# A split adaLN product: eight chunks ahead of the first norm, the others between the chunks of other matrices, in four strips of 32 columns

## What is computed

```python
c_act = jax.nn.silu(c)
for i in range(DEPTH):
    mod = (c_act @ ada_w[i] + ada_b[i])[:, None, :]          # (1024) @ (1024, 6144)
    sh1, sc1, g1, sh2, sc2, g2 = jnp.split(mod, ADA_CHUNKS, axis=-1)
    h = _rmsnorm(x, norm_mix_g[i]) * (1.0 + sc1) + sh1
    m = _conformer_conv(h, ...) if i == 0 else _stick_breaking_attention(h, ...)
    x = x + g1 * m
    h = _rmsnorm(x, norm_ffn_g[i]) * (1.0 + sc2) + sh2
    x = x + g2 * _peer(h, pk_w_q[i], pk_keys[i], pk_u[i], pk_v[i])
return _rmsnorm(x, final_g)
```

## Time and profile before

| | us |
|---|---|
| median of 3 runs | 3544.87 (3542.72 to 3547.4) |
| the profiled execution | 3545.07 |
| its span in the trace | 3543.3 |
| busy in the span: PE, DVE, POOL, ACT | 3179.2, 2502.8, 1254.0, 479.0 |
| mean granted TensorE clock | 0.921 |

### The profile page before, as it was taken

How to read it: one execution, slowest core, us unless ns; L and a number is a source line. 1 busy time by engine, 2 the same in 40 slices (tenths; PEclk the granted TensorE clock), 3 DMA queues, 4 the chain that set the end, 5 groups by cost and what they waited for, 6 DMA issues and landing times.

```text
span 3543.3 us, 44528 instructions
## 1 busy us (share of the span) xinstructions
PE 3179.2 (90%) x12852; PEld 2291.5 (65%) x12852; DVE 2502.8 (71%) x5303; ACT 479.0 (14%) x1062; POOL 1254.0 (35%) x1168
## 2 busy tenths in 40 slices
PE   7899869699999999999979897838999999999996
PEld 3685746596776766555568784737877676655554
DVE  0397899778888886666623586397788888766665
ACT  0211211010000000000043215201100000000001
POOL 0000000105555557777500000002255555677773
PEclk9899979659999999999979999975699999999998
DMA  8234315319999999999922340213399999999996
GB/s 313 87 133 170 114 64 180 131 32 388 410 403 409 406 406 410 410 410 410 372 84 97 118 143 12 85 59 100 114 410 407 406 401 409 405 410 410 410 410 262
DMA packets 242900, 957.18 MB, mean 270 GB/s; under 512 B 26953, under 2 KB 27129, under 8 KB 225146
## 3 DMA queue, kind: packets, MB, share of 16 engines
q0 software_dynamic: 147456, 536.94, 38.5%
q1 hardware_dynamic: 95354, 419.17, 31.2%
HBM read 953.90 MB, written 2.10 MB: 270 GB/s over the span
## 4 chain that ended last, share of the span: by engine, by line
PE 53%; DMA 16%; issue 12%; DVE 11%; ACT 4%; POOL 3%; DVEq 0%; POOLq 0%; ACTq 0%; SPq 0%
DMA v_rows<-in_pk_v,idx_now 14%; PE out_e L727 13%; PE acc L718 13%; PE acc L488 11%; PE mid L708 6%; PE acc L480 4%; DVE mod_rows L1290 2%; POOL v_rows L426 1%; DVE scratch L1309 1%; POOL u_rows L420 1%; DMA u_rows<-in_pk_u,idx_now 1%; PE mid L679 1%; PE out_e L510 1%; DMA weights<-in_ada 1%; DVE scratch L1306 1%
## 5 line engine op out<-in xcount | busy, mean ns | idle before, releaser
L727 PE MATMUL out_e<-weights,mod_rows 128*128 128x512 f32 x2048 | 932.4, 598 | 61.6 <-DVE mod_rows L1335 59.7
L718 PE MATMUL acc<-h_t,weights 128*128 128x256 f32 x4096 | 933.8, 381 | 0.0
L718 PEld LDWEIGHTS acc<-h_t,weights 128*128 128x128 f32 x4096 | 784.0, 192 | 217.8 <-issue 123.5
L426 POOL DMA_INDIRECT v_rows<-in_pk_v,idx_now x512 | 630.5, 1231 | 606.0 <-DVE mod_rows L1290 484.9
L1290 DVE SCALAR_TENSOR_TENSOR mod_rows<-v_rows,acts,mod_rows 128x1024 f32<-128x1024 f32 x512 | 657.9, 1285 | 199.0 <-DMA v_rows<-in_pk_v,idx_now 195.5
L1273 DVE SCALAR_TENSOR_TENSOR u_rows<-u_rows,h_rows 128x1024 f32<-128x1024 f32 x512 | 625.8, 1222 | 82.5 <-DMA u_rows<-in_pk_u,idx_now 81.7
L727 PEld LDWEIGHTS out_e<-weights,mod_rows 128*128 128x128 f32 x2048 | 377.2, 190 | 468.1 <-issue 368.0
L420 POOL DMA_INDIRECT u_rows<-in_pk_u,idx_now x512 | 564.6, 1103 | 292.4 <-issue 142.3
L415 POOL COPY idx_now<-pick_idx 128x8 int32 (+1 forms) x128 | 56.2, 439 | 1348.2 <-DVE pick_gate L1268 1300.5
L708 PEld LDWEIGHTS mid<-scratch 128*128 128x128 f32 x2048 | 338.6, 257 | 20.2 <-DVE scratch L1309 16.9
L708 PE MATMUL mid<-scratch 128*128 128x64 f32 x2048 | 341.4, 343 | 10.6 <-DVE scratch L1309 10.6
(11 more groups left out here) (184 smaller groups left out, 2072.0 us busy)
## 6 DMA issues: line engine op xcount, KB each, us to landing
weights<-in_u_t SPq DMA_DIRECT2D x256, 512.0 KB, 6.7
weights<-in_pk_v SPq DMA_DIRECT2D x256, 512.0 KB, 6.7
weights<-in_ada SPq DMA_DIRECT2D x42, 1024.0 KB, 4.9
weights<-in_pk SPq DMA_DIRECT2D x32, 1024.0 KB, 4.8
weights<-in_w_qkv SPq DMA_DIRECT2D x24, 1024.0 KB, 4.8
weights<-in_w_in SPq DMA_DIRECT2D x16, 1024.0 KB, 4.8
weights<-in_w_out SPq DMA_DIRECT2D x8, 1024.0 KB, 4.9
u_rows<-in_pk_u,idx_now POOLq DMA_INDIRECT x512, 10.9
```

The costliest lines, as they stand in the source:

```text
L426: nc.gpsimd.indirect_dma_start(v_rows[:, r % VR, :], None, a["pk_v"], bass.IndirectOffsetOnAxis(ap=idx_now[:, 1, par, r:r + 1], axis=0)).t ...
L718: last = nc.tensor.matmul(acc[s][:, 0:HALF], weights[:, s, k * P:(k + 1) * P], h_t[:, k, :], start=k == 0, stop=k == KB - 1)
L727: last = nc.tensor.matmul(out_e[2 * tt + c][:, :], e_act[:, s, tt * P:(tt + 1) * P], weights[:, s, D + c * 512:D + (c + 1) * 512], start=F ...
```

## The change

**The product in four strips.** `c_pad` is widened to windows of 32 columns, and `ada_rows` to all 128 partitions. The eight matmuls of a chunk no longer go to the same 24 rows: number `k` goes to the strip of 32 rows that begins at `k % 4 * 32`, by `tile_position`, so that row `n` of each of four strips gets a quarter of the sum of chunk `n`. The four are added where they are used: `strips`, a 128x32 tile that DVE makes once out of `ident`, takes the place of `ident` in `spread_columns` and in the picks of `spread_rows`, whose matmuls then run over 128 rows and not 24. The bias comes in by one matmul ahead of ACT's copy (`ada_bias_in`), and DVE's addition is gone.

**Layer 0 in two parts.** The first eight chunks (shift and scale of the first norm) stand ahead of everything: two through `weights`, six through `u_rows` and `v_rows`, whose DMAs SP now issues all at once, around the load of `x`. The other 16 stand two by two behind each `glu` chunk of half 0, in another PSUM tile (`out_e[1]`); their columns and rows are spread behind the second `glu` chunk of half 1.

**Layer 1 one by one.** Its 24 chunks stand each behind one chunk of `out` half 0 (4), `pk` half 0 (8), `out` half 1 (4) and `pk` half 1 (8), and none are left behind the last `pk`. DVE makes `mod_cols` of layer 1 behind the seventh `rank` of half 1, with the first softmax.

```diff
-ASIDE = 6
-ADA_PIECES = ((0, 4), (4, 4), (8, 2), (10, 2), (12, 12))
+STRIP = 32
+STRIPS = P // STRIP
+NOW = 8
+ASIDE = NOW - 2
-CHAIN = ([("ada", 0, 0, range(ADA_CHUNKS - ASIDE)),
-          ("glu", 0, 0, range(8)), ("glu", 0, 1, range(8)), ("ada", 1, 0, range(0, 4)), ("ada", 1, 1, range(4, 8)),
-          ("out", 0, 0, range(3)), ("ada", 1, 2, range(8, 10)), ("out", 0, 0, range(3, 4)), ("ada", 1, 3, range(10, 12)),
-          ("pk", 0, 0, range(8)), ("out", 0, 1, range(4)), ("pk", 0, 1, range(8)), ("ada", 1, 4, range(12, 24)),
+def beside(stage, half, count, first):
+    return [c for i in range(count) for c in ((stage, 0, half, i), ("ada", 1, 0, first + i))]
+CHAIN = ([("ada", 0, 0, 0), ("ada", 0, 0, 1)] +
+         [c for i in range(8) for c in (("glu", 0, 0, i), ("ada", 0, 0, NOW + 2 * i), ("ada", 0, 0, NOW + 2 * i + 1))] +
+         [("glu", 0, 1, i) for i in range(8)] +
+         beside("out", 0, 4, 0) + beside("pk", 0, 8, 4) + beside("out", 1, 4, 12) + beside("pk", 1, 8, 16) +
...
-            def ada_chunk(l, n, chunk):
-                window = ADA_CHUNKS - 1 - n
+            def ada_chunk(n, chunk, to, first):
+                window = STRIP - 1 - n
                 for k in range(KB):
-                    last = nc.tensor.matmul(out_e[0][0:ADA_CHUNKS, 0:NC], c_pad[:, k, window:window + ADA_CHUNKS],
-                                            chunk[:, k * NC:(k + 1) * NC], start=n + k == 0,
-                                            stop=n == ADA_CHUNKS - 1 and k == KB - 1)
+                    at = k % STRIPS * STRIP
+                    last = nc.tensor.matmul(to[at:at + STRIP, 0:NC], c_pad[:, k, window:window + STRIP],
+                                            chunk[:, k * NC:(k + 1) * NC], start=first and k < STRIPS, stop=False,
+                                            tile_position=(0, at))
...
             pe.wait_ge(c_pad_ready, 1)
-            ada(0, 0, ADA_CHUNKS - ASIDE)
+            for n in range(2):
+                ada(0, n, out_e[0], n == 0)
             for i in range(ASIDE):
                 pe.wait_ge(aside_in[i], 16)
-                last = ada_chunk(0, ADA_CHUNKS - ASIDE + i, aside[i])
+                last = ada_chunk(2 + i, aside[i], out_e[0], False)
             last.then_inc(aside_used, 1)
-            spread_columns(0)
+            ada_bias_in(0, out_e[0])
+            spread_columns(0, mid[0])
...
-            for i in range(4):
+            for i in range(8):
+                if i == 4:
+                    norm(0, 1, 0)
                 by_channel("glu", 0, 0, i)
-            norm(0, 1, 0)
-            spread_rows(0)
-            for i in range(4, 8):
-                by_channel("glu", 0, 0, i)
+                for n in range(NOW + 2 * i, NOW + 2 * i + 2):
+                    ada(0, n, out_e[1], n == NOW)
+            ada_bias_in(1, out_e[1])
             normed_columns(0, 1, 0)
             for i in range(8):
                 by_channel("glu", 0, 1, i)
+                if i == 1:
+                    spread_columns(1, mid[1])
+                    spread_rows(0)
             pe.wait_ge(rows_ready, 8)
             means(0, range(4))
-            ada(1, 0, 4)
             variance(0)
-            ada(1, 4, 4)
-            for i in range(3):
+            for i in range(4):
                 conv_out(0, i)
-            ada(1, 8, 2)
-            conv_out(0, 3)
-            ada(1, 10, 2)
+                ada(1, i, out_e[0], i == 0)
             norm(0, 0, 1)
             select(0, 0, {1: lambda: means(1, range(4)), 3: lambda: variance(1)})
             for i in range(4):
                 conv_out(1, i)
+                ada(1, 12 + i, out_e[0])
             norm(0, 1, 1)
             select(0, 1)
-            ada(1, 12, 12)
-            spread_columns(1)
+            ada_bias_in(2, out_e[0])
+            spread_columns(2, mid[0])
             peer(0)
```

More of the change, by code:

```diff
@@ L515, in ada @@
-            def ada(l, first, count):
-                if l and first == 0:
-                    pe.wait_ge(rows_ready, 8 * l)
-                for n in range(first, first + count):
-                    at = NUMBER["ada", l, 0, n]
-                    pe.wait_ge(weights_in[at % 2], 16 * (at // 2 + 1))
-                    ada_chunk(l, n, weights[:, at % 2, :]).then_inc(ada_used, 1)
-            def spread_columns(l):
-                pe.wait_ge(ada_ready, l + 1)
+                    at = k % STRIPS * STRIP
@@ L526, in spread_columns, with ada_bias_in @@
+            def ada_bias_in(part, to):
+                pe.wait_ge(bias_in, 32 if part == 2 else 16)
+                nc.tensor.matmul(to[:, 0:NC], ident[0:ADA_CHUNKS, :], ada_bias[:, :], start=False, stop=True
+                                 ).then_inc(ada_full, 1)
+            def spread_columns(part, to):
+                pe.wait_ge(ada_ready, part + 1)
+                pe.wait_ge(strips_ready, 1)
                 for c in range(2):
-                    last = nc.tensor.matmul(mid[0][:, c * ADA_CHUNKS:(c + 1) * ADA_CHUNKS], ada_rows[:, c * P:(c + 1) * P],
-                                            ident[0:ADA_CHUNKS, 0:ADA_CHUNKS], start=True, stop=True)
+                    last = nc.tensor.matmul(to[:, c * ADA_CHUNKS:(c + 1) * ADA_CHUNKS], ada_rows[:, c * P:(c + 1) * P],
+                                            strips[:, 0:ADA_CHUNKS], start=True, stop=True)
@@ L836, in norm @@
             def norm(l, h, which):
[L837 removed]
+                act.wait_ge(mod_ready, 3 if l else 1 + which)
                 act.wait_ge(rstd_ready, norm_no(l, h, which, 0) // 2 + 1)
```

107 lines of the change are left out of this document (55 added, 52 removed).

## The result

The changed kernel takes 3604.96 us (median of four executions, 3602.66 to 3606.15), against 3545.45 us for the kernel before in the same comparison (3542.72 to 3547.4): the ratio is 1.0168, 95% interval 1.0150 to 1.0185. It is 59.5 us slower. Direction and mechanism were forecast, the size (36 us) was not.

A forecast was written before the change was run, and what follows sets the result against it. Loads and adaLN products bound the start, then DVE's convolution and ranks; 83 us gained in front was to be lost in longer steps, `peer(0)` starting at 698.3 instead of 662.22: 3545 + 36 = 3581 us, range 3557 to 3605.

The forecast's parts named there:

- The front: Ahead of the first `glu` product: loads decide, and `glu` starts at 44.5 us instead of 127.76, 83 us ahead.
- a: PE's price of one adaLN chunk in four strips: taken as 1.8 us, between 0.9 side by side and 3.54 serial.
- A load whose place comes free late costs 5.0 us, the next one 2.6 more: Beside adaLN chunks: a load issued when its slot frees lands 5.0 us later; in `glu` the next load adds 2.6.
- The clock, 1.2 us a `glu` and `out` step and 1.5 in `pk`: PE returns slow after each load wait: 1.2 us added per `glu` and `out` step, 1.5 per `pk` step.
- the clock doesn't fall: Rival: no clock loss in the `glu`, `pk` and `out` steps and first scores, 25 us less, 3557 to 3562; chance 0.2.
- `out` of half 0 is covered by DVE, 2 us show: Layer 0, `out` of half 0: steps of 14.8 us, mostly hidden by DVE's half blocks between residuals; 2 us show.
- `pk` steps 13.4: `pk` of half 0: each step 6.91 + 5.0 + 1.5 = 13.4 us instead of 7.80; eight steps 109.6 instead of 71.8.
- First scores and ranks: `pk` of half 1: first scores after 25.9 us instead of 17.7; then DVE's ranks bind, 124.7 less 1.6 to `peer(0)`.
- Behind `peer(0)` nothing over 3 us: From 662 us on, after `peer(0)` starts: no term over 3 us, the rest follows as a block.
- The signs: Expected in the changed profile: `glu` steps 15 to 16 us, `centre` at 240 to 255, `peer`'s output at 680 to 720.
- hidden gaps (3517): Rival: exposed load gaps in `glu`, `pk` and `out` steps stay hidden, a chunk costing its 2.6 us transfer: 3517; chance 0.08.
- The fourth: Rival: strips run one after the other at 3.54 us a chunk and the clock falls in each gap: 3605 us; chance 0.17.

The follow-up runs named there:

- filled to the brim: Changed kernel with more matmuls of unread result added in the load gaps of layer 0's `glu`, `out` and `pk` steps: 3563.6 us.
- first experiment: Changed kernel with the eight products of an adaLN chunk put into one strip of 32 rows, one after the other: 3589.65 us.
- the kernel with the spare tiles: Changed kernel with adaLN chunks behind the second loaded through idle `u_rows`/`v_rows` tiles, layer 1's chunks distributed differently: 3477.15 us.
- one-strip version: The kernel with the spare tiles, but with the eight products of each adaLN chunk in one strip: 3577.04 us.
- the strips at their old places: Changed kernel with both layers' adaLN chunks back in the old order, keeping the four-strip product and what comes with it: 3501.97 us.

## Why the prediction came out as it did

**The front** (44.5 forecast, 45.99 measured): right. The eight chunks are bound by their loads; a = 1.07 instead of 1.8 changes nothing there.

**A load whose place comes free late costs 5.0 us, the next one 2.6 more**: right. The chain shows 4.6 to 5.0 us for `in_pk` and `in_w_out` (6.0 once), and in `glu` PE is back on a product 7.4 us after the last one ended (55.08 to 62.48; 7.3 to 8.4 in the others).

**The clock, 1.2 us a `glu` and `out` step and 1.5 in `pk`: this is the step that failed.** The mechanism was right, its price too low. I took it from one place, where 32 adaLN matmuls stood behind a wait of 2.96 us. In the changed kernel the eight `glu` products took 8.66 to 9.50 us, 9.17 in the mean, against 7.17 at full clock, so 2.0 (and the sum's base, 6.91, holds only for products in a row: 0.2 more a step); an `out` chunk took 11.85 us from its bias matmul at 295.82 to its adaLN chunk at 307.67, where it takes 8.55 with the gaps filled, so 3.3; a `pk` product 8.6 to 8.9 (and 10.08 once), mostly, so 1.7. Against the forecast that is 0.8 x 8 in `glu` and 0.4 to 2.1 in each `out` chunk, 12 to 13 in the seven on the path (three of half 0, four of half 1): about 19 of the 22.4 us; it is what grew in the table in the rows behind `glu` and behind the two `out`. The rival "the clock doesn't fall" put the sum's clock terms at 25 us (they make 27 on the path); taking the clock's fall away (filled to the brim) measured 39, and left 20 us over the kernel before, where that rival had 12 to 17.

The argument for the rival was wrong too: that adaLN products cut the gaps in two spoke, as I put it, for the full clock. At 1.07 us they are too short to do that. At 3.64 us they do (first experiment), which is why the one-strip kernel is faster: the tiling and the filling order work against each other. The Trainium skill, "TensorE: Matmul & The Clock Gate", section "HAM oscillation — how this bites in real kernels", describes the mechanism as throttling between bursts of matmuls separated by waits on DMA. The trace agrees: the granted clock is 0.81 in the `glu` steps, and 0.96 in the one-strip kernel and in the one filled to the brim (117 to 179 us). The bursts of that section are shorter than its waits; here they are longer, 8.7 to 9.5 us against some 4, and the clock fell all the same.

**`out` of half 0 is covered by DVE, 2 us show**: too little. With steps of 16.9 us DVE waited 22.6 us for four products (1.53, 3.28, 15.55 and 2.20) where it had waited 14.2, so 8.3 showed; 6.2 us of delay grew in that stage.

**`pk` steps 13.4**: right where a wait stood in them (13.7 to 13.9 in the last steps of half 0). Behind the means and the variance the load was hidden and the product ran at full clock, which the sum did not have, and the one at 406.71 ran at full clock too; so half 0 took 106.8 in all for 109.6. **First scores and ranks**: right; from `pk` of half 1 to the first `rank` 27.3 us for 25.9, and from there 122.8 for 123.1.

**Behind `peer(0)` nothing over 3 us**: right, 1.4.

**The signs.** The waits for `in_pk` and `in_w_out` came as described in all but two steps, DVE's for `region` too, and its waits for `out` of half 1 were 14.8 to 16.3 us, but 0.88 once. The `glu` steps were 16.3 to 17.5 us and not 15 to 16, `centre` came at 257.79 and not by 255, and `peer`'s output at 720.65, just outside 680 to 720: the same underpriced term in each.

The other rivals: hidden gaps (3517) and an even result didn't occur. The fourth, 3605 with serial strips and the clock falling in every gap, gave the measured time, but not for its reason: the strips did run side by side (3.3 times as fast), and a kernel with serial strips took 3590.

What stays open: the share of the 67 us that belongs to layer 1's other order in the kernel with the spare tiles, which was not tried alone (its `v_rows` hold the scores of half 1, so chunks beside `pk` of half 1 can't use them); whether one ring with more slots would do as well as separate tiles; and why the profiled run of the strips at their old places was 12 us over its timed ones.

## What to carry to other kernels

Interleaving two streams through one ring of two slots turns prefetch two ahead into none: each load is then released by the instruction just ahead of its use, and costs its whole latency (here 5 us for 1 MB, where bandwidth asks 2.6). Before interleaving, follow for one load which instruction frees its place; give the second stream a place of its own (128 us here), or alternate in pairs (26 us). A short product in a gap does not keep PE's clock up, so making the work in a gap faster can make the kernel slower, as it did here by 15 us; judge it together with the wait that it stands in.

## What the runs showed of the hardware

- **Four 32-column strips, float32, 128x256:** 16 records in 1.07 us instead of 3.54 (3.64 through windows of 32 columns in one strip), 3.3 to 3.4 times as fast. Two chunks in a row start 1.86 us ahead of the next product (102.19 to 104.05 in the kernel with the spare tiles) where they take 7.03 in one strip (58.53 to 65.56 in its one-strip version), 3.8 times as fast. The Trainium skill, "TensorEngine Tiling (Array Packing)", section "Theoretical Speedup", gives up to four; the runs stay a little below.
- **The clock behind a wait is not the same each time.** In `pk` of half 0, products behind waits of 2.7 to 4.0 us took 8.86 us, but the one at 406.71, behind 2.78 us, took 7.17.
- **Products whose result nobody reads cost nothing while PE would wait.** 388 records on `c_pad` (90.5 us of PE) made the kernel 39 us faster, and the loads of `out` did not slow down: from the start of an adaLN chunk to PE's start on the next `out` chunk it took 4.9 to 5.2 us with them and 4.8 to 5.1 without, with 0.2 to 0.5 us of wait left.
